# Pieces' loads before the last weights' loads, one layer's tables in two chunks, and the order of y's last products

## The reference

```python
for l in range(DEPTH):                                   # DEPTH = 2
    mod = (cs @ ada_w[l] + ada_b[l]).reshape(bn, N_SUB, 3, D_MODEL)
    shift, scale, gate = mod[:, :, 0, None], mod[:, :, 1, None], mod[:, :, 2, None]
    u = x * (1.0 + scale[:, 0]) + shift[:, 0]
    y = _swiglu(u, ffn_w13[l, 0], ffn_w2[l, 0])          # (silu(a) * g) @ w2, width 2816
    x = _layer_norm(ALPHA * x + 0.5 * gate[:, 0] * y, ln_g[l, 0], ln_b[l, 0])
    u = x * (1.0 + scale[:, 1]) + shift[:, 1]
    y = _hybrid_mixer(u, ...)                            # four kinds of token mixer, side by side
    x = _layer_norm(ALPHA * x + gate[:, 1] * y, ln_g[l, 1], ln_b[l, 1])
    u = x * (1.0 + scale[:, 2]) + shift[:, 2]
    y = _swiglu(u, ffn_w13[l, 1], ffn_w2[l, 1])
    x = _layer_norm(ALPHA * x + 0.5 * gate[:, 2] * y, ln_g[l, 2], ln_b[l, 2])
```

## Time and profile before

| what | us |
|---|---|
| median of 3 runs | 1121.89 (1119.5 to 1122.13) |
| the profiled execution | 1117.89 |
| its span, first to last instruction | 1115.2 |
| PE busy | 1049.0 (94%) |
| DVE busy | 907.3 (81%) |
| ACT busy | 423.0 (38%) |
| chain that ended last | PE 67%, DVE 17%, DMA 4%, PEld 4%, issue 3%, ACT 3% |
| mean granted TensorE clock | 0.985 |

### The profile page before, as it was taken

The page is one execution under the profiler, slowest core; times in us unless marked ns, Lnnn a source line. Parts: engine busy times, 40 slices in busy tenths (PEclk is TensorE's granted clock), DMA queues, the critical chain, the costliest instruction groups (busy, mean ns, idle before and its releaser), DMA issues.

```text
span 1115.2 us, 17047 instructions
## 1 busy us (share of the span) xinstructions
PE 1049.0 (94%) x6885; PEld 917.9 (82%) x6885; DVE 907.3 (81%) x1523; ACT 423.0 (38%) x574; POOL 34.9 (3%) x56
## 2 busy tenths in 40 slices
PE   1999999999959999999999999999999999999995
PEld 1889989987845699999988988998787569999994
DVE  6888999979858899889879998699897688755555
ACT  0445334323532443333333553331337244333331
POOL 1000000003000000000000000000300000000000
PEclk9999999989989999999999999999999999999998
DMA  9899998852353678888957987787335247564540
GB/s 369 284 316 326 304 305 295 283 143 77 97 205 119 214 260 315 310 299 306 329 178 247 314 278 227 255 312 196 114 95 186 76 161 262 182 217 146 204 152 38
DMA packets 184585, 250.84 MB, mean 225 GB/s; under 512 B 25452, under 2 KB 133296, under 8 KB 183484
## 3 DMA queue, kind: packets, MB, share of 16 engines
q1 hardware_dynamic: 184508, 249.76, 66.0%
HBM read 248.69 MB, written 1.05 MB: 224 GB/s over the span
## 4 chain that ended last, share of the span: by engine, by line
PE 67%; DVE 17%; DMA 4%; PEld 4%; issue 3%; ACT 3%; SPq 1%; PEldq 0%; POOL 0%; POOLq 0%; DVEq 0%; ACTq 0%
PE PS L616 11%; PE PS L617 11%; PE PS L615 11%; PE PS L639 5%; PE PS L643 5%; PE PS L642 5%; PE PS L734 5%; DVE w_in_lo L1131 3%; PEld PS L734 3%; PE PS L960 2%; DMA xn<-in_ada_w_dram 2%; DVE acc L1063 2%; DVE w_out_lo L1136 1%; DMA w_in_ring<-in_ffn_w_dram 1%; DVE qk_tanh L1063 1%
## 5 line engine op out<-in xcount | busy, mean ns | idle before, releaser
L617 PE MATMUL PS<-u_hi,w_in_lo 128*128 128x256 f32 x1280 | 359.9, 281 | 0.0
L616 PE MATMUL PS<-u_lo,w_in_hi 128*128 128x256 f32 x1280 | 359.1, 281 | 0.0
L615 PE MATMUL PS<-u_hi,w_in_hi 128*128 128x256 f32 x1280 | 358.8, 280 | 0.0
L615 PEld LDWEIGHTS PS<-u_hi,w_in_hi 128*128 128x128 f32 x1280 | 241.7, 189 | 1.8
L616 PEld LDWEIGHTS PS<-u_lo,w_in_hi 128*128 128x128 f32 x1280 | 240.5, 188 | 1.6
L617 PEld LDWEIGHTS PS<-u_hi,w_in_lo 128*128 128x128 f32 x1280 | 240.2, 188 | 0.0
L1131 DVE TENSOR_TENSOR w_in_lo<-w_in_ring,w_in_hi 128x2048 fp32r<-128x2048 f32 x88 | 201.2, 2289 | 27.5 <-ACT w_in_hi L1774 27.4
L1774 ACT ACTIVATE w_in_hi<-w_in_ring 128x2048 fp32r<-128x2048 f32 x88 | 168.0, 1913 | 4.3 <-DMA w_in_ring<-in_ffn_w_dram 4.3
L1767 ACT ACTIVATE arena<-PS 128x256 f32<-128x256 f32 x88 | 33.8, 384 | 292.2 <-PE PS L617 270.6
L639 PE MATMUL PS<-w_out_hi,h_parts 128*128 128x512 f32 x320 | 131.8, 412 | 5.7 <-DVE h_parts L1125 5.7
L1785 ACT ACTIVATE w_out_hi<-w_out_ring 128x1024 fp32r<-128x1024 f32 x80 | 80.6, 1055 | 133.5 <-PE PS L643 133.5
(11 more groups left out here) (314 smaller groups left out, 1262.3 us busy)
## 6 DMA issues: line engine op xcount, KB each, us to landing
w_in_ring<-in_ffn_w_dram SPq DMA_DIRECT2D x88, 1024.0 KB, 7.7
arena<-in_ada_w_dram SPq DMA_DIRECT2D x30, 2048.0 KB, 8.4
w_out_ring<-in_ffn_w_dram SPq DMA_DIRECT2D x44, 1024.0 KB, 6.4
w_in_ring<-in_w_in_dram SPq DMA_DIRECT2D x6, 1024.0 KB, 6.8
w_in_ring<-in_w_in_dram SPq DMA_DIRECT2D x10, 512.0 KB, 5.1
w_out_ring<-in_w_out_dram SPq DMA_DIRECT2D x4, 1024.0 KB, 8.5
w_in_ring<-in_w_in_dram SPq DMA_DIRECT2D x2, 2048.0 KB, 8.8
w_in_ring<-in_w_out_dram SPq DMA_DIRECT2D x4, 1024.0 KB, 5.9
```

The costliest lines, as they stand in the source:

```text
L615: pe.matmul(y, hi, u_hi[:, kt, :], start=(i == 0), stop=False)
L616: pe.matmul(y, hi, u_lo[:, kt, :], start=False, stop=False)
L617: mm = pe.matmul(y, lo[:, kt, half, :], u_hi[:, kt, :], start=False, stop=(i == KT - 1))
```

## The change

Three edits, with no change of what is computed.

In SP's order for the mixer, load_ada_pair(0) with its wait now stands ahead of load_last_out, and load_ffn_in stands behind the wait for conv_step and load_ada_pair(1). The wait for conv_step stands there in both layers.

The table steps of layer 1 stand in chunk 5 (k = 0 to 4) and chunk 6 (k = 5 and 6). Layer 0 keeps its places.

In the last chunk of all four FFNs, PE starts with (c, 0, 0) and (c, 0, 1), and all products of token tile 1 follow: first the 12 matmuls of column half 0 (chunk c-1, then c), then the 12 of half 1.

```diff
--- before.py
+++ after.py
@@ -464,17 +464,17 @@
                     load_mix_out(m)
                 for m in range(2, 5):
                     load_mix_in(m)
-                load_last_out()
-                slot2 = G_FFN2 % 2
-                load_ffn_in(l, 1, slot2, 0, ring_use(l, G_FFN2))
                 if l == 0:
                     sp.wait_ge(sem("sb_ready"), l + 1)
                     waited(sp)
                     load_ada_pair(0)
+                load_last_out()
                 sp.wait_ge(sem("conv_step"), l * 12 + 12)
                 waited(sp)
                 if l == 0:
                     load_ada_pair(1)
+                slot2 = G_FFN2 % 2
+                load_ffn_in(l, 1, slot2, 0, ring_use(l, G_FFN2))
                 sp.wait_ge(sem("cols_turned"), l + 1)
                 waited(sp)
                 sp.wait_ge(sem("g_spread"), l + 1)
@@ -628,11 +628,11 @@
                     else:
                         spread_gate(n)
 
-                def out_part(c, tt, ft):
+                def out_part(c, tt, ft, halves=range(2)):
 
                     slot = ff_group(f, c) % 2
                     parts, his = (h_parts_last, w_out_hi_last) if c == CHUNKS - 1 else (h_parts, w_out_hi)
-                    for hf in range(2):
+                    for hf in halves:
                         tok, cols = slice(tt * P, (tt + 1) * P), slice(hf * 512, (hf + 1) * 512)
                         h_hi, h_lo = parts[:, 2 + ft, tok], parts[:, ft, tok]
                         y = PS[:, 2 * tt + hf, :]
@@ -646,17 +646,16 @@
                         elif (tt, ft, hf) == (1, 1, 1):
                             mm.then_inc(sem(f"w_out_used{slot}"), 1)
 
-                if last:
-                    out_part(c - 1, 1, 0)
                 for tt, ft in ((0, 0), (0, 1)) if c >= CHUNKS - 2 else ((0, 0), (1, 0), (0, 1), (1, 1)):
                     if tt == 0:
                         pe.wait_ge(sem("w_out_split"), tile + (ft + 1))
                         pe.wait_ge(sem("h_done"), tile + (ft + 3))
                     out_part(c, tt, ft)
                 if last:
-                    out_part(c - 1, 1, 1)
-                    out_part(c, 1, 0)
-                    out_part(c, 1, 1)
+                    for hf in range(2):
+                        for made in (c - 1, c):
+                            for ft in range(2):
+                                out_part(made, 1, ft, (hf,))
 
             def release_out(slot):
 
@@ -1349,8 +1348,9 @@
                             v.wait_ge(sem("rot_step"), at + 4)
                             v.tensor_tensor(sin_t[:, :, hi], t4[2], t4[3], ALU.add).then_inc(sem("rot_step"), 1)
 
-                TABLE_AT = {3: ((0, range(6)), (1, range(6))), 4: ((2, range(6)), (3, range(6))), 5: ((4, range(6)),),
-                            6: ((5, range(6)),), 7: ((6, range(0, 3)),), 8: ((6, range(3, 6)),)}
+                steps = lambda *ks: tuple((k, range(6)) for k in ks)
+                TABLE_AT = ({3: steps(0, 1), 4: steps(2, 3), 5: steps(4), 6: steps(5), 7: ((6, range(0, 3)),), 8: ((6, range(3, 6)),)},
+                            {5: steps(0, 1, 2, 3, 4), 6: steps(5, 6)})[l]
 
                 for c in range(CHUNKS - 1):
                     ffn_chunk(l, 0, c)
```

## The result

| kernel | median us | executions | profiled execution | its span | mean clock |
|---|---|---|---|---|---|
| before | 1120.7 | 4 (1118.73 to 1122.13) | 1117.89 | 1115.2 | 0.985 |
| after | 1105.94 | 4 (1105.07 to 1107.58) | 1105.07 | 1102.6 | 0.988 |

The ratio is 0.9871, with a 95% interval of 0.9849 to 0.9893: the kernel is 14.8 us faster than before by these medians. 1107.4 was forecast, and the range of 1102.5 to 1112.0 holds the time.

What follows compares the result with a forecast made beforehand. PE, busy 94%, was taken as the bound, with an 11.61 us hole from a late DMA on the path. Gains of 13.1 - 0.9 + 1.0 + 0.4 + 0.9 = 14.5 us took 1121.89 to 1107.4; range 1102.5 to 1112.

Steps and rivals of the forecast that it cites:

- Bound and hole: Layer 0's mixer: DVE waits 11.9 us on piece 0, leaving PE idle; without it the scores start 11.7 us earlier.
- no DMA wait on DVE in layer 0's mixer: Sign expected in the profile after, with piece 0 issued near 294 and piece 1 near 308.
- The clock: Layer 0's scores: without the hole the clock stays up and they take 1.66 us, not 3.06; 1.4 us gained.
- The first rival: Layer 0's clock falls ahead of y_tile as in layer 1; loads give 10.7 us, not 13.1; time 1109.8; chance 0.28.
- part 1: Layer 0's mixer, earlier piece loads: 11.7 us from the hole plus 1.4 from the clock, 13.1 us gained.
- Part 2: Layer 1's first FFN, moved table steps: PE's waits for hidden values shrink; 2.4 us if made alone.
- Part 3: FFN ends, y's last products: 0.9 and 1.4 us lost at first FFNs, 0.4 and 0.9 gained at second ones.
- The step that failed: End of layer 0's second FFN: DVE starts 1.4 us earlier, the turn waited only 0.34 us for it; 0.4 gained.
- The sum of 14.5: Whole kernel: 13.1 - 0.9 + 1.0 + 0.4 + 0.9 us gained, set against the median of 1121.89.
- The other rivals: Layer 0's mixer: piece 1 late by 1.9 us, 1109.3, chance 0.08; FFN-2 weights late behind conv_step, near 1130, chance 0.01.

Runs made afterwards that it cites:

- the 15 dummies: Kernel before, with 15 dummy matmuls between y_tile and PE's wait in layer 0's mixer; one execution 1117.1 us, beside 1116.98 for before.
- part 1 alone: Kernel before with only SP's new order of the piece loads; median 1107.87 us, ratio 0.9899 to before.
- after once more: The changed kernel, unaltered, measured and profiled a second time; median 1104.32 us, ratio 0.9853 to before.
- best_busy: Changed kernel with y's new order in second FFNs only, plus more dummies between adaLN sums behind each first FFN; 1099.42 us, ratio 0.9824 to before.
- parts 1 and 2: Kernel before with SP's new load order and layer 1's moved table steps, y's products in the old order; 1102.14 us, ratio 0.9851.

## Why the prediction was right

**Bound and hole.** The reading held: one DMA wait, behind the FFN-2 weights in SP's queue, on the path. It gave 11.68 us where 11.7 stood in the sum. The scores were expected 16.5 us after attention (321.6 - 305.14) and came after 16.50. Pieces 0 and 1 were issued 2.6 and 2.3 us behind "near 294" and "near 308", since the stages ahead are 2.5 us longer (+0.84 + 1.86 - 0.23). Piece 0 landed 13 us before it was wanted, where "some 15" stood, and piece 1 landed 6.0 us after its issue, at 316.3, 1.7 us before DVE came to it; the 8.0 us that were counted for it had left no margin (315.8 against 315.6). The sign "no DMA wait on DVE in layer 0's mixer" was put too wide: the three short ones behind 347 were there before as well.

**The clock.** 1.4 us were forecast, 1.42 seen, and 1.5 with the 15 dummies. In the windows of after the clock is at 1.00 (2.4 GHz) at 321 and 325, around y_tile and the scores: without the hole it stayed up. At 237 and 770 it is at 0.50 (1.2 GHz), though PE is 100% busy in both, with the small matmuls behind the first FFNs. The columns are those of the earlier trace rows:

```profile
237.00:238.00 1.00, 1.00 (x4) 0.53 (x3) 0.32 (x2) 0.00 (x0) 0.55 (x1) 0.50 1.04 414
321.00:322.00 1.00, 0.46 (x7) 0.22 (x2) 1.00 (x5) 1.00 (x5) 0.00 (x0) 1.00 1.07 367
325.00:326.00 1.00, 1.00 (x11) 0.88 (x9) 0.18 (x1) 1.00 (x4) 0.00 (x0) 1.00 1.08 372
770.00:771.00 1.00, 1.00 (x6) 1.00 (x7) 0.00 (x0) 1.00 (x2) 0.00 (x0) 0.50 1.07 418
```

**The first rival**, with a chance of 0.28, wasn't the case in the profile of after and was in two others (part 1 alone, after once more), where part 1 gave 10.2 and 10.4 us against the 10.7 worked out. I had put it as a question of which kernel; it is one of which execution. Of the seven profiles with both pieces ahead of the FFN-2 weights, five show no fall there. In these two the fall behind the first FFN is missing, and in best_busy alone of the others. The Trainium skill, page "TensorE: Matmul & The Clock Gate", section "What's actually happening", calls the window in which activity is judged free-running, and gives that as the reason why the point at which the clock is first released varies from run to run. The trace shows more than that: a later fall of layer 0 lay at 237 to 247 in one execution of the changed kernel and at 317 to 324 in the other. That activity releases the throttle, as the same section of the Trainium skill has it, doesn't cover the fall at 770, where PE was busy all the time.

**Part 2.** 2.4 us forecast, 2.16 measured (2.14 with part 1). By chunk 9 layer 1 was 13.47 us ahead of before (755.34 against 741.87), 10.80 of it from what came earlier: 2.7 us, where 2.6 was worked out. The wait in chunk 9 is down from 0.97 to 0.41 as put (0.4). No wait of PE for h_parts appeared in chunks 6 and 7. Behind chunk 9 some 0.5 us of it is given back, where the working had 0.2: PE now waits 0.46 us for the last hidden values (the line of parts 1 and 2 above), which before it didn't. The mechanism stands, and the size of that last term was off.

**Part 3.** On its own a loss of 1.0 us was worked out, and the stages of after give a loss of 1.3: +0.84 in layer 0's first FFN (1.0 over its last chunk alone; 0.9 forecast, with PE idle 0.83 where 0.8 was expected), +1.4 in layer 1's against parts 1 and 2 alone (1.4 forecast, idle 1.85 for "about 2"), -0.18 in layer 0's second (0.4 forecast), -0.79 at the end (0.9 forecast). In layer 1's first FFN the recorded sum is off by 0.1: 36 products from 767.45 on end at 775.8, and before y's last one starts at 776.43 and so is over by 776.66: 0.9 us ahead and not 1.0; 0.74 was measured. Deepnorm started 0.55, 1.38, 2.1 and 0.72 us earlier than before in the four, shifts taken out, where 0.5, 1.4, 2.3 and 0.9 stood. The starts of three of them, before and then after:

```profile
228.58 1.29 DVE L1175 TENSOR_TENSOR xn<-PS,gate_bc 128x512 f32<-128x512 f32 x2 [1.85 <-PE PS L643]
...
772.09 1.29 DVE L1175 TENSOR_TENSOR xn<-PS,gate_bc 128x512 f32<-128x512 f32 x2 [1.49 <-PE PS L643]
...
1096.95 1.29 DVE L1175 TENSOR_TENSOR xn<-PS,gate_bc 128x512 f32<-128x512 f32 x2 [1.96 <-PE PS L643]
```

```profile
228.03 1.29 DVE L1174 TENSOR_TENSOR xn<-PS,gate_bc 128x512 f32<-128x512 f32 x2 [1.43 <-PE PS L643]
...
759.16 1.29 DVE L1174 TENSOR_TENSOR xn<-PS,gate_bc 128x512 f32<-128x512 f32 x2 [1.49 <-PE PS L643]
...
1084.40 1.29 DVE L1174 TENSOR_TENSOR xn<-PS,gate_bc 128x512 f32<-128x512 f32 x2 [1.22 <-PE PS L643]
```

**The step that failed** is "the turn at 580.57 waited for it only 0.34 us beyond PE's own sums: 0.4 us gained". The turn did come earlier (569.45, with no idle time ahead of it, 0.49 us earlier with the shift of 10.63 taken out). But the modulation of the turned x needs the last adaLN sum, which is PE's own work and which nothing moved. DVE now waits 1.37 us for it and PE then 0.87 for u_lo instead of 0.52. The timelines of DVE and PE after:

```profile
569.62 0.17 DVE L1072 TENSOR_TENSOR mod<-PS,abT 128x16 f32<-128x16 f32 x1 [1.37 <-PE PS L550]
```

```profile
572.04 0.36 PE L577 MATMUL PS<-u_hi,w_in_hi 128*128 128x256 f32 x1 [0.87 <-DVE u_lo L1092]
```

Before, that step came at 580.27 and PE's at 582.84:

```profile
580.27 0.17 DVE L1073 TENSOR_TENSOR mod<-PS,abT 128x16 f32<-128x16 f32 x1
```

```profile
582.84 0.35 PE L577 MATMUL PS<-u_hi,w_in_hi 128*128 128x256 f32 x1 [0.52 <-DVE u_lo L1093]
```

With the shift, 580.27 is 569.64: the same place. So the stage gave 0.18 us (0.15 in the kernel with part 3 in the second FFNs only) and not 0.4. I had asked what the turn waits for and not what its result waits for.

**The total.** The sum of 14.5 was made on one execution and came out as 12.6 there. Part 1 gave its 13.1, and parts 2 and 3 gave 0.9 where 1.4 stood (-0.84 + 0.74 + 0.18 + 0.79). The rest lies in the stages in which the clock fell in one of the two profiles or for longer in one: they took 1.6 us more from the block turns to attention in layer 0 and 2.6 more in layer 1, and gave back 2.9 in layer 1's mixer, where the clock no longer fell. The medians differ by 14.8, because the profiled execution of before is 2.8 us below its median and that of after 0.9. The forecast's base moved too: it was the median of three executions, 1121.89, and with the fourth it is 1120.7, from which a gain of 14.5 gives 1106.2. So how near the forecast lies (1107.4 against 1105.94) is in part luck: where the clock falls moves a single span by some us (4.3 between the profiles of part 1 and of parts 1 and 2), and the sum knew nothing of it.

**The other rivals.** Piece 1 wasn't late (0.47 us of idle time ahead of its steps, for DVE's own step). The wait for conv_step in front of load_ffn_in was passed at 310 and the FFN-2 weights were issued at 317.78, with layer 0's second FFN at 191.76 us for 191.79 before: no cost.

## What to carry to other kernels

When an engine waits once and long on a DMA, look in the queue's timeline for what was issued ahead of it and isn't wanted for long, and move every load that the chain wants next in front of it: one piece alone only hands the wait on to the next. Work that is ready covers a wait for what isn't. In this kernel giving it up paid only where another engine set the end, so such an order is to be applied by stage and not in all of them. And for a gain that is worked out by an earlier start, follow the result of the started step to its next operand as well.

## What the runs showed of the hardware

The place of the clock's fall isn't a property of the kernel: two executions of the changed one differ in it. Behind layer 0's first FFN it fell in 11 of the 14 profiles, from 235 to 238, and stayed at 0.50 for 6.8 or 10.2 us; the stage from block turns to z took 7.49 us without a fall (8.42 with the added dummies) and up to 11.19 with one. Behind layer 1's first FFN it fell in 9 of 14. Whether it also falls ahead of y_tile seems to hang together with it (it did in two of the three profiles in which it hadn't fallen behind the first FFN, and in none of the eleven others), but no run here makes it fall at will, so this stays open. In layer 1 it leans the same way: the clock fell in its mixer in four of the five profiles without a fall behind its first FFN, and in three of the nine with one.

What a load of 512 KB behind 2 MB costs depended on which 2 MB stood ahead. By the DMA view (issue to landing) it landed after 7.9 us, and the next piece after 7.5, behind the last w_out tiles, whose two loads took 6.1 us in the median; behind the FFN-2 weights of the kernel before, whose two took 7.8, it landed after 9.7.

A dummy of 384 columns in 32-bit floats took 0.65 us at the full clock (two records), nearly three times the 0.23 us of a 512-column matmul of the FFN, whose split operands the kernel holds as fp32r (DVE's rows write h_parts so). The two 512-column matmuls of y_tile, in plain 32-bit floats too, took 1.98 us in four records.
